# Causal attention with relative bias on the paired helpers, in a two-block fp32 transformer kernel

## The chip, the cores and the metric

The kernel runs on one core of one Trainium2 chip. The metric is device time in microseconds of one execution of the whole program; the figure for a kernel is the median of its runs.

## What is computed

Two transformer blocks of two layers each, over 256 tokens of width 1024 (the first block adds 16 meta tokens), all in fp32. The part that the change touches is the attention of the second block's first layer, named MoBA. With 256 tokens and blocks of 256 its selection of other blocks selects nothing, and what remains is causal attention of 16 heads of width 64 over the own block, with a relative bias:

```python
q, k, v = jnp.split(h @ w_qkv, 3, axis=-1)      # 16 heads of 64
...
l_own = ... jnp.einsum(... qf, k_own) * scale
d_own = t[:, None] - (j_own * BLK + jnp.arange(BLK))[None, :]
b_own = jnp.moveaxis(bias_table[rel_bucket(d_own)].astype(jnp.float32), -1, 0)
l_own = jnp.where((d_own >= 0)[None], l_own + b_own, NEG)
p = jax.nn.softmax(jnp.concatenate([l_sel, l_own], axis=-1), axis=-1)
...
return o @ w_o
```

Around it the layer is `x = x + moba_attention(rms_norm_2(x, g))`, then `x = x + square(relu(rms_norm_2(x, g) @ w_up)) @ w_down`.

## The kernel before

Everything is held transposed: features on the 128 partitions, tokens along the row. A linear layer is cut into output tiles of 128 features. One tile takes its weights as one piece of 128 x 1024, and for each of its eight chunks of 128 input features three matmuls: high part times high part, high times low, low times high (`pe_tile`, lines 304 to 306). `pe_linear` runs the tiles of one layer; the table `LINEARS` is the order of all layers, and each engine runs through it in that order (`ORDER`).

Weights go through a ring of four slots. SyncE loads a piece into `raw`; ACT rounds it to `w_hi` (`act_round`, line 256), which needs the piece four before it to be used up by PE (`piece_used`); DVE computes the remainder `w_lo` (`dve_rest`, line 265); then PE may use it. While tile t is computed, ACT and DVE prepare piece t + 3. Results lie in four PSUM banks in turn (`tile_bank`), and a tile waits until DVE has read the tile that had its bank (`evac_done`).

In a layer that ends in a residual (`RESID`, such as `moba_out`) DVE does, for each tile t: remainder of piece t + 3, add of tile t to `h` (`dve_resid`, line 429), `x_lo` of tile t - 1. ACT does, for each tile: rounding of piece t + 3, then `x_hi` of tile t (`act_resid`, `act_x_hi`, line 378). GpSimd sums squares for the next norm. The next layer's first tile takes its chunks as their `x_lo` arrives.

`moba_in` is the layer of queries, keys and values: 24 tiles, and tiles 3p, 3p + 1, 3p + 2 are the queries, keys and values of heads 2p and 2p + 1, stored by DVE to `qm`. The attention is woven into these tiles by `att_pe`, `att_dve` and `att_act` (class `Attend`), head by head: in step u PE computes the scores of head u (line 1281), one or two projection tiles (`MOBA_SIDES`), the transposes of the probabilities of head u - 2 (line 1241) and the values of head u - 3 (line 1266). Between, DVE adds the bias and takes the maximum (line 1325), ACT computes the exponentials (line 1376), DVE multiplies by the reciprocal sum (lines 1340, 1343), and ACT copies the transposes to `pt_m` (line 1394). Value rows are transposed once a pair (line 1934) into the free half of bank 6 and copied by ACT (line 1913). After every second head ACT writes `y_hi` (line 1407) and DVE `y_lo` (line 1361), the inputs of the output projection `moba_out`. The scores use banks 5 and 7, the transposes bank 4, the values bank 6. When the 24 tiles are used up, scores of heads 14 and 15 and what follows them run with no tile beside them, and `moba_out` begins behind the last values.

The first block's sliding-window attention (`swa_in`, `pe_swa`) uses another set of helpers, class `Pairs`: the two heads of a pair lie on partitions 0 to 63 and 64 to 127, and their scores are issued alternately, into banks 2 and 3 (`pair_scores`, line 1448); so are their values, into the two halves of the partitions of bank 6 (`pair_values`, line 1470). Its projection tiles use two banks, 0 and 1. In the last step it computes the first six chunks of two tiles of its output projection ahead (`SWA_EARLY`).

## Times and profile before

| | us |
|---|---|
| median of 3 runs | 1376.86 (1376.09 to 1377.64) |
| the profiled execution | 1382.77 |
| its span | 1381.0, granted TensorE clock 0.966 |
| PE busy, DVE busy, ACT busy in it | 1305.0, 898.7, 660.9 |

The profile is of one execution. The page gives for each engine how long it was busy, the chain of work that ended last, and the costliest groups of instructions by line. The trace behind it can be asked for the instructions of an engine in order of time, and for the busy time and granted clock of a stretch. PE shows overlapping matmuls: the distance of their starts is what one costs, not their duration. An fp32 matmul stands as two records. The stage of the change runs from 744 us, where `moba_in` starts, to 858 us, where `moba_out` starts, and `moba_out` ends at 885 us.

### The profile page before, as it was taken

How to read it: one execution, taken by the hardware profiler on the slowest of the kernel's cores; microseconds unless marked ns; L12 is line 12 of the kernel's file. 1: busy time of each engine (PE TensorE's matmuls, PEld its weight loads, DVE VectorE, ACT ScalarE, POOL GpSimd, SP SyncE). 2: the span in 40 equal slices, each digit the busy share in tenths (PEclk: the TensorE clock that was granted, in tenths of full speed). 3: DMA queues.
4: the chain of work that ended last, by engine and by line, in shares of the span. 5: the costliest groups of instructions: out<-in, count | busy, mean ns of one | idle time of the engine just before them, and what ended most of it. 6: DMA issues, size and time to landing. Idle time of an engine off the chain costs nothing.

```text
span 1381.0 us, 27358 instructions
## 1 busy us (share of the span) xinstructions
PE 1305.0 (94%) x10217; PEld 1245.8 (90%) x10217; DVE 898.7 (65%) x1681; ACT 660.9 (48%) x1148; POOL 185.2 (13%) x233
## 2 busy tenths in 40 slices
PE   7988989999999989999999998999999878999996
PEld 6968979999999869899999986999999766999996
DVE  6956337887755675888755664777555687776553
ACT  5544224555533554655544443555444266555431
POOL 4112213000012222000011000300011123200011
PEclk9979989999999998999999998999999999999998
DMA  6423804555654312555656432565556521555551
GB/s 232 155 90 67 133 16 137 173 178 169 207 176 136 108 62 92 178 185 183 207 190 199 138 122 74 159 189 187 184 185 195 181 68 33 181 183 184 187 191 64
DMA packets 60354, 206.31 MB, mean 149 GB/s; under 512 B 6000, under 2 KB 14320, under 8 KB 60144
## 3 DMA queue, kind: packets, MB, share of 16 engines
q1 hardware_dynamic: 56000, 200.81, 46.1%
q10 hardware_dynamic: 4272, 4.35, 1.0%
q8 instruction: 58, 0.95, 0.3%
q14 instruction: 24, 0.20, 0.0%
HBM read 200.95 MB, written 4.19 MB: 149 GB/s over the span
## 4 chain that ended last, share of the span: by engine, by line
PE 83%; DVE 10%; ACT 4%; issue 3%; POOL 1%; DMA 0%; DVEq 0%; POOLq 0%; ACTq 0%
PE bank L304 24%; PE bank L306 24%; PE bank L305 24%; DVE w_lo L265 3%; ACT w_hi L256 2%; DVE cb L635 1%; PE bank L1266 1%; PE bank L1078 1%; PE bank L1281 1%; PE bank L1094 1%; PE bank L1032 1%; PE bank L1092 1%; DVE sm_d L1325 1%; PE bank L1241 1%; DVE x_lo L383 1%
## 5 line engine op out<-in xcount | busy, mean ns | idle before, releaser
L265 DVE TENSOR_TENSOR w_lo<-raw,w_hi 128x1024 fp32r<-128x1024 f32 (+1 forms) x358 | 458.8, 1282 | 244.3 <-ACT w_hi L256 244.1
L256 ACT ACTIVATE w_hi<-raw 128x1024 fp32r<-128x1024 f32 (+1 forms) x358 | 388.2, 1085 | 315.7 <-PE bank L306 292.6
L304 PE MATMUL bank<-x_hi,w_hi 128*128 128x256 f32 (+2 forms) x1784 | 519.9, 291 | 18.3 <-DVE x_lo L383 13.9
L306 PE MATMUL bank<-x_hi,w_lo 128*128 128x256 f32 (+2 forms) x1784 | 511.4, 287 | 0.0
L305 PE MATMUL bank<-x_lo,w_hi 128*128 128x256 f32 (+2 forms) x1784 | 511.2, 287 | 0.0
L304 PEld LDWEIGHTS bank<-x_hi,w_hi 128*128 128x128 f32 x1784 | 341.1, 191 | 28.3 <-DVE w_lo L265 11.8
L306 PEld LDWEIGHTS bank<-x_hi,w_lo 128*128 128x128 f32 x1784 | 341.4, 191 | 0.0
L305 PEld LDWEIGHTS bank<-x_lo,w_hi 128*128 128x128 f32 x1784 | 340.7, 191 | 0.3
L304 PE MATMUL bank<-m_hi,w_hi 128*128 128x256 f32 x512 | 143.4, 280 | 0.0
L305 PE MATMUL bank<-m_lo,w_hi 128*128 128x256 f32 x512 | 142.8, 279 | 0.0
L306 PE MATMUL bank<-m_hi,w_lo 128*128 128x256 f32 x512 | 142.8, 279 | 0.0
L304 PE MATMUL bank<-a_hi,w_hi 128*128 128x272 f32 (+1 forms) x352 | 100.1, 284 | 0.0
L305 PE MATMUL bank<-a_lo,w_hi 128*128 128x272 f32 (+1 forms) x352 | 99.9, 284 | 0.0
L306 PE MATMUL bank<-a_hi,w_lo 128*128 128x272 f32 (+1 forms) x352 | 99.8, 284 | 0.0
L304 PE MATMUL bank<-y_hi,w_hi 128*128 128x256 f32 (+2 forms) x312 | 93.3, 299 | 4.9 <-DVE y_lo L2026 1.7
L306 PEld LDWEIGHTS bank<-m_hi,w_lo 128*128 128x128 f32 x512 | 96.3, 188 | 0.0
L304 PEld LDWEIGHTS bank<-m_hi,w_hi 128*128 128x128 f32 x512 | 96.1, 188 | 0.0
L305 PEld LDWEIGHTS bank<-m_lo,w_hi 128*128 128x128 f32 x512 | 95.7, 187 | 0.0
L378 ACT ACTIVATE x_hi<-h,prm 128x272 fp32r<-128x272 f32 x64 | 32.7, 521 | 125.2 <-DVE h L429 125.2
L305 PE MATMUL bank<-y_lo,w_hi 128*128 128x256 f32 (+2 forms) x312 | 91.6, 294 | 0.0
L306 PE MATMUL bank<-y_hi,w_lo 128*128 128x256 f32 (+2 forms) x312 | 91.3, 293 | 0.0
L397 POOL TENSOR_TENSOR acc<-h 128x272 f32<-128x272 f32 x9 | 5.8, 642 | 637.2 <-DVE h L429 631.9
(298 smaller groups left out, 1767.2 us busy)
## 6 DMA issues: line engine op xcount, KB each, us to landing
raw<-w_up SPq DMA_DIRECT2D x88, 512.0 KB, 3.5
raw<-w_mlp_up SPq DMA_DIRECT2D x64, 512.0 KB, 4.3
raw<-w_mlp_down SPq DMA_DIRECT2D x64, 512.0 KB, 4.1
raw<-w_down SPq DMA_DIRECT2D x32, 704.0 KB, 4.0
raw<-w_mix_in SPq DMA_DIRECT2D x29, 512.0 KB, 3.5
raw<-w_moba_in SPq DMA_DIRECT2D x24, 512.0 KB, 3.5
raw<-w_swa_in SPq DMA_DIRECT2D x12, 512.0 KB, 3.5
raw<-w_mix_out SPq DMA_DIRECT2D x8, 512.0 KB, 3.9
```

The source lines that it names most:

```text
L256: nc.scalar.activation(w_hi[:, slot, 0:WIDTHS[g]], raw[:, slot, 0:WIDTHS[g]], ACT.Copy).then_inc(hi_ready, 1)
L265: nc.vector.tensor_tensor(w_lo[:, slot, 0:WIDTHS[g]], raw[:, slot, 0:WIDTHS[g]], w_hi[:, slot, 0:WIDTHS[g]].bitcast(F32), ALU.subtract).th ...
L304: nc.tensor.matmul(out, whi, xh, start=(chunk == 0), stop=False)
L305: nc.tensor.matmul(out, whi, xl, start=False, stop=False)
L306: mm = nc.tensor.matmul(out, wlo, xh, start=False, stop=end)
L378: nc.scalar.activation(x_hi[:, c, :], h[:, c, :], ACT.Copy, scale=norm_w(name, c)).then_inc(x_hi_ready, 1)
L383: nc.vector.scalar_tensor_tensor(out=x_lo[:, c, :], in0=h[:, c, :], scalar=norm_w(name, c), in1=x_hi[:, c, :].bitcast(F32), op0=ALU.mult, ...
L635: nc.vector.scalar_tensor_tensor(out=cb[:, t % 2, :], in0=g[:, tap:tap + T], scalar=dn_w(tap, t + 4 * i), in1=cb[:, t % 2, :], op0=ALU.mul ...
L1032: nc.tensor.matmul(BC[b % 4][:, 0:T], ident[0:rows, col:col + 1].to_broadcast([rows, P]), (ba if b < 8 else l2r)[0:rows, :], start=True, s ...
L1078: mm = nc.tensor.matmul(pbank[0:c, hs], bt[0:c, n, hs], xm_of(n)[0:c, hs], start=True, stop=True)
L1092: nc.tensor.matmul(half(INV_BANKS[n][1][0:c, hs], level, 0), xt_of(n)[0:c, hs], half(p[0:c, hs], level, 0), start=True, stop=True)
L1094: mm = nc.tensor.matmul(half(yt_bank(n)[0:c, hs], level, 1), p[0:c, hs], half(xt_of(n)[0:c, hs], level, 1), start=True, stop=True)
```

## The change

The class of MoBA's attention changes from `Attend` to `Pairs`, and the engines' code for `moba_in` is written out on the paired helpers.

- `tile_bank`: the tiles of `moba_in` use two banks, 0 and 1, in place of four; a tile waits for the read of the tile two before it.
- Eight steps, one a pair. PE: scores of both heads, transposes of the pair's value rows (now in bank 7), two tiles, transposes of both heads' probabilities of the same pair, one tile, values of both heads.
- DVE: bias and maximum of both heads, `y_lo` of the pair before, read of the first tile, normalisation of both heads, then remainders and reads of the other tiles. ACT: `y_hi` of the pair before, value rows, exponentials of both heads, two roundings, two copies of transposes, one rounding.
- The last step has no tiles of `moba_in`. There PE computes seven of eight chunks (`MOBA_EARLY`) of tiles 0, 1 and 2 of `moba_out` between the parts of the attention; `pe_linear` adds the eighth chunk of each, then goes on with tile 3.

```diff
-            if lin is LIN["swa_in"]:
+            if lin in (LIN["swa_in"], LIN["moba_in"]):
                 return bank[(lin.tile0 + t) % 2]
...
-                behind = 2 if lin is LIN["swa_in"] else BANKS
+                behind = 2 if lin in (LIN["swa_in"], LIN["moba_in"]) else BANKS
...
-            begun = 2 if name == "swa_out" else 0
+            begun, chunk = {"swa_out": (2, SWA_EARLY), "moba_out": (3, MOBA_EARLY)}.get(name, (0, 0))
             for t in range(begun):
-                pe_tile(pe, lin, t, ready=ready if t == 0 else None, part=(SWA_EARLY, KD))
+                pe_tile(pe, lin, t, ready=ready if t == 0 else None, part=(chunk, KD))
...
-            att_dve(dve, moba, tile=tile)
+            for p in range(HEADS // 2):
+                t = 3 * p + 3
+                more = t < lin.tiles
+                pair_reduce(dve, moba, p)
+                if p:
+                    pair_low(dve, moba, p - 1)
+                if more:
+                    tile(t)
+                pair_norm(dve, moba, p)
+                if more:
+                    rest(t)
+                    tile(t + 1)
+                    rest(t + 1)
+                    rest(t + 2)
+                    tile(t + 2)
+            pair_low(dve, moba, HEADS // 2 - 1)
...
+            round_(0)
+            act_std(act, name)
+            round_(1)
+            round_(2)
+            for p in range(HEADS // 2):
+                t = 3 * p + 3
+                more = t < lin.tiles
+                if p:
+                    pair_high(act, moba, p - 1)
+                act.wait_ge(S("mv_turned"), p + 1)
+                nc.scalar.activation(vrow_m[:, :, p * P:(p + 1) * P],
+                                     bank[7][:, 0:SEQ].rearrange("p (c k) -> p c k", c=2),
                                      ACT.Copy).then_inc(S("mv_ready"), 1)
...
+                pair_exps(act, moba, p)
+                if more:
+                    round_(t)
+                    round_(t + 1)
+                pair_copies(act, moba, p)
+                if more:
+                    round_(t + 2)
+            pair_high(act, moba, HEADS // 2 - 1)
...
+            def value_turn(p):
+                pe.wait_ge(evac_done, lin.tile0 + 3 * p + 3)
+                if p:
+                    pe.wait_ge(S("mv_ready"), p)
...
-            att_pe(pe, moba, tile=lambda t: pe_tile(pe, lin, t), rows=rows)
+            for p in range(HEADS // 2):
+                t = 3 * p + 3
+                pe.wait_ge(evac_done, lin.tile0 + 3 * p + 2)
+                pair_scores(pe, moba, p)
+                value_turn(p)
+                if t < lin.tiles:
+                    pe_tile(pe, lin, t)
+                    pe_tile(pe, lin, t + 1)
+                    pair_turn(pe, moba, p)
+                    pe_tile(pe, lin, t + 2)
+                    pe.wait_ge(S("mv_ready"), p + 1)
+                    pair_values(pe, moba, p)
+                else:
+                    pe_tile(pe, out, 0, ready=early, part=(0, MOBA_EARLY))
+                    moba.wait(pe, "max", 2 * HEADS)
+                    pe_tile(pe, out, 1, part=(0, MOBA_EARLY))
+                    pair_turn(pe, moba, p)
+                    pe_tile(pe, out, 2, part=(0, 4))
+                    pe.wait_ge(S("mv_ready"), p + 1)
+                    pair_values(pe, moba, p)
+                    pe_tile(pe, out, 2, part=(4, MOBA_EARLY))
```

PE's row at the change of one pair to the next, before (values of head 0, value rows of the second pair, transposes of head 1, scores of head 4, then a tile):

```order
L1266 MATMUL bank<-pt_m,vrow_m 64x256
L1266 MATMUL bank<-pt_m,vrow_m 64x128
L1934 MATMUL bank<-cst,qm 128x128 x2
L1241 MATMUL bank<-cst,sm_m 128x128 x3
L1281 MATMUL bank<-qm 128x256
L1281 MATMUL bank<-qm 128x128
L304 MATMUL bank<-x_hi,w_hi 128x256
```

The same place in the changed kernel:

```order
L1470 MATMUL bank<-pt_m,vrow_m 64x256 x2
L1470 MATMUL bank<-pt_m,vrow_m 64x128 x2
L1448 MATMUL bank<-qm 128x256 x2
L1448 MATMUL bank<-qm 128x128 x2
L1955 MATMUL bank<-cst,qm 128x128 x2
L304 MATMUL bank<-x_hi,w_hi 128x256
```

Values and scores now stand for two heads each, side by side, once in three tiles; the six transposes (line 1460) stand alone between the second and third tile.

DVE's row in one step of the changed kernel, from the second head's scores on (1515 is `y_lo`, 1884 and 1888 read a tile, 265 is a weight remainder):

```order
L1493 TENSOR_SCALAR st_m<-st_m 128x2
L1515 TENSOR_TENSOR y_lo<-bank,y_hi 128x256
L1884 SCALAR_TENSOR_TENSOR qm<-bank,rstd 128x256
L1500 RECIPROCAL st_m<-st_m 128x2
L1509 TENSOR_SCALAR sm_m<-sm_m,st_m 128x256
L1509 TENSOR_SCALAR sm_m<-sm_m,st_m 128x128
...
L265 TENSOR_TENSOR w_lo<-raw,w_hi 128x1024
L1888 TENSOR_TENSOR qm<-bank,rstd 128x256
L265 TENSOR_TENSOR w_lo<-raw,w_hi 128x1024 x2
L1888 TENSOR_TENSOR qm<-bank,rstd 128x256
```

And before, in a step with two tiles:

```order
L1331 TENSOR_SCALAR st_m<-st_m 128x2
L1340 RECIPROCAL st_m<-st_m 128x2
L1343 TENSOR_SCALAR sm_m<-sm_m,st_m 128x256
L1343 TENSOR_SCALAR sm_m<-sm_m,st_m 128x128
L1889 SCALAR_TENSOR_TENSOR qm<-bank,rstd 128x256
L265 TENSOR_TENSOR w_lo<-raw,w_hi 128x1024
L1893 TENSOR_TENSOR qm<-bank,rstd 128x256
L265 TENSOR_TENSOR w_lo<-raw,w_hi 128x1024
```

Before, a remainder followed each read; now the read of the first tile stands ahead of both heads' normalisation, and two remainders stand ahead of the read of the third tile.

PE's row behind the last tile of `moba_in`, before, from the scores of head 15 on:

```order
L1281 MATMUL bank<-qm 128x256
L1281 MATMUL bank<-qm 128x128
L1266 MATMUL bank<-pt_m,vrow_m 64x256
L1266 MATMUL bank<-pt_m,vrow_m 64x128
L1934 MATMUL bank<-cst,qm 128x128 x2
L1241 MATMUL bank<-cst,sm_m 128x128 x6
...
L304 MATMUL bank<-y_hi,w_hi 128x256
L305 MATMUL bank<-y_lo,w_hi 128x256
L306 MATMUL bank<-y_hi,w_lo 128x256
```

And now, from the scores of the last pair on:

```order
L1448 MATMUL bank<-qm 128x256 x2
L1448 MATMUL bank<-qm 128x128 x2
L1955 MATMUL bank<-cst,qm 128x128 x2
L304 MATMUL bank<-y_hi,w_hi 128x256
...
L1460 MATMUL bank<-cst,sm_m 128x128 x6
L304 MATMUL bank<-y_hi,w_hi 128x256
...
L1470 MATMUL bank<-pt_m,vrow_m 64x256 x2
L1470 MATMUL bank<-pt_m,vrow_m 64x128 x2
L304 MATMUL bank<-y_hi,w_hi 128x256
```

Matmuls of the output projection (`y_hi`) moved ahead of the last pair's transposes and values: 14 chunks ahead of the transposes, four between them and the values, three behind.

## Rows read from the trace of the kernel before

**Rows 1.** Windows: stretch, its length, busy PE, PEld, DVE, ACT, POOL, clock, DMA

```profile
750.00:840.00 90.00, 90.00 (x668) 81.46 (x667) 56.63 (x160) 44.75 (x101) 0.00 (x0) 1.00 0.43 142
850.00:860.00 10.00, 8.28 (x28) 5.37 (x29) 1.50 (x3) 2.71 (x6) 0.00 (x0) 0.50 0.00 0
555.00:560.00 5.00, 4.26 (x20) 3.69 (x21) 4.07 (x5) 4.18 (x5) 1.61 (x2) 0.75 0.48 137
```

**Rows 2.** PE timeline, one pair's period: start, us, line, idle before

```profile
774.65 0.86 PE L1266 MATMUL bank<-pt_m,vrow_m 128*64 128x256 f32 x4
775.45 0.44 PE L1934 MATMUL bank<-cst,qm 128*128 128x128 f32 x2
...
776.14 0.92 PE L1281 MATMUL bank<-qm 64*128 64x256 f32 x4
776.99 0.39 PE L304 MATMUL bank<-x_hi,w_hi 128*128 128x256 f32 x1
...
779.94 0.49 PE L1241 MATMUL bank<-cst,sm_m 128*128 128x128 f32 x3
...
789.33 0.92 PE L1281 MATMUL bank<-qm 64*128 64x256 f32 x4
```

**Rows 3.** DVE timeline of the output projection: remainders and residual adds

```profile
859.35 1.23 DVE L265 TENSOR_TENSOR w_lo<-raw,w_hi 128x1024 fp32r<-128x1024 f32 x1 [0.52 <-ACT w_hi L256]
862.54 0.43 DVE L429 TENSOR_TENSOR h<-bank,h 128x256 f32<-128x256 f32 x1 [1.97 <-PE bank L306]
864.51 1.23 DVE L265 TENSOR_TENSOR w_lo<-raw,w_hi 128x1024 fp32r<-128x1024 f32 x1 [1.54 <-ACT w_hi L256]
865.65 0.42 DVE L429 TENSOR_TENSOR h<-bank,h 128x256 f32<-128x256 f32 x1
...
884.72 0.41 DVE L429 TENSOR_TENSOR h<-bank,h 128x256 f32<-128x256 f32 x1
```

**Rows 4.** PE timeline behind both output projections, the sliding-window one first

```profile
555.57 0.39 PE L304 MATMUL bank<-x_hi,w_hi 128*128 128x258 f32 x1 [2.54 <-DVE x_lo L383]
...
558.26 0.41 PE L304 MATMUL bank<-x_hi,w_hi 128*128 128x256 f32 x1
558.90 0.41 PE L304 MATMUL bank<-x_hi,w_hi 128*128 128x256 f32 x1
...
885.60 0.39 PE L304 MATMUL bank<-x_hi,w_hi 128*128 128x256 f32 x1 [1.12 <-DVE x_lo L383]
```

**Rows 5.** PE timeline in the sliding-window stage: paired values, scores, transposes

```profile
476.46 0.87 PE L1470 MATMUL bank<-pt_s,vrow 128*64 128x256 f32 x8
477.26 0.70 PE L1767 MATMUL bank<-ptx,vmbd 128*128 128x256 f32 x2
477.89 0.97 PE L1448 MATMUL bank<-qs 64*128 64x272 f32 x8
478.79 0.88 PE L1460 MATMUL bank<-cst,sm_s 128*128 128x128 f32 x6
479.51 0.38 PE L1762 MATMUL bank<-cst,smx 128*128 128x128 f32 x2
...
505.30 0.97 PE L1448 MATMUL bank<-qs 64*128 64x272 f32 x8
```

**Rows 6.** PE timeline: start of projection tile 2, last chunk of tile 23

```profile
750.00 0.28 PE L304 MATMUL bank<-x_hi,w_hi 128*128 128x256 f32 x1
...
840.11 0.28 PE L304 MATMUL bank<-x_hi,w_hi 128*128 128x256 f32 x1
```

**Rows 7.** DVE timeline: a sliding-window pair's last normalisation, read of tile 0

```profile
510.07 0.54 DVE L1509 TENSOR_SCALAR sm_s<-sm_s,st_s 128x256 f32<-128x256 f32 x2
...
749.77 0.42 DVE L1889 SCALAR_TENSOR_TENSOR qm<-bank,rstd 128x256 f32<-128x256 f32 x1
```

**Rows 8.** ACT timeline: the last y_hi and the rounding behind it

```profile
857.99 0.38 ACT L1407 ACTIVATE y_hi<-bank 128x256 fp32r<-128x256 f32 x1 [1.63 <-PE bank L1266]
858.27 1.05 ACT L256 ACTIVATE w_hi<-raw 128x1024 fp32r<-128x1024 f32 x1
```

More of the change, by code:

```diff
@@ L1844, in build @@
             ("qm", [P, 24, SEQ]), ("vrow_m", [P, 2, D]), ("bias_m", [P, HEADS, 2 * P]),
-            ("sm_m", [P, 3, 3 * P]), ("pt_m", [P, 2, 3 * P]), ("st_m", [P, HEADS, 10])], u_at)
+            ("sm_m", [P, 4, 3 * P]), ("pt_m", [P, 2, 2, 3 * P]), ("st_m", [P, HEADS, 8])], u_at)
         CAUSAL_TURNS = ((4, 0, P, 2 * P), (4, P, P, 0), (4, 2 * P, P, P))
-        MOBA_SIDES = {}
-        for pair in range(1, HEADS // 2):
-            MOBA_SIDES[2 * pair - 2] = (3 * pair, 3 * pair + 1)
-            MOBA_SIDES[2 * pair - 1] = (3 * pair + 2,)
-        moba = Attend(
-            "moba", "moba_out", 2 * P, P,
-            lambda u, r, g: qm[r, u // 2, P * g:P * (g + 1)],
-            lambda u, r, g: qm[r, 8 + u // 2, 0:P * (g + 1)],
-            lambda u, chunk, c: vrow_m[:, chunk, u * HD:(u + 1) * HD],
-            lambda u: bias_m[:, u, :], lambda u: bias_m[:, u, P:2 * P], CAUSAL_TURNS,
-            (sm_m, pt_m, st_m), MOBA_SIDES)
+        MOBA_EARLY = 7
+        moba = Pairs(
+            "moba", "moba_out", 2 * P, P, 0, 0,
+            lambda p, r, g: qm[r, p, P * g:P * (g + 1)],
+            lambda p, r, g: qm[r, 8 + p, 0:P * (g + 1)],
+            lambda p, j, chunk: vrow_m[:, chunk, (2 * p + j) * HD:(2 * p + j + 1) * HD],
+            lambda u: bias_m[:, u, :], lambda u: bias_m[:, u, P:2 * P], lambda u, x: 1.0,
+            (sm_m, pt_m, st_m))
         def load_bias(act, dst):
@@ L1894, in tile, with rest @@
                                             ALU.mult).then_inc(evac_done, 1)
+            def rest(t):
                 dve_rest(dve, lin.piece0 + t + AHEAD)
@@ L1906, in act_moba, with round_ @@
             lin = LIN[name]
-            def tile(t):
+            def round_(t):
                 act_round(act, lin.piece0 + t + AHEAD)
-            def rows(pair):
-                act.wait_ge(S("mv_turned"), pair + 1)
-                nc.scalar.activation(vrow_m[:, :, pair * P:(pair + 1) * P],
-                                     bank[6][:, SEQ:2 * SEQ].rearrange("p (c k) -> p c k", c=2),
-                                     ACT.Copy).then_inc(S("mv_ready"), 1)
-            tile(0)
-            act_std(act, name)
@@ L1919, in act_moba @@
-            tile(1)
-            tile(2)
-            att_act(act, moba, tile, rows)
+            round_(0)
[10 more added lines that the diff above has]
+                                     bank[7][:, 0:SEQ].rearrange("p (c k) -> p c k", c=2),
+                                     ACT.Copy).then_inc(S("mv_ready"), 1)
+                pair_exps(act, moba, p)
[5 more added lines that the diff above has]
+                    round_(t + 2)
@@ L1923, in pe_moba @@
+            pair_high(act, moba, HEADS // 2 - 1)
         def pe_moba(pe, name):
             lin = LIN[name]
-            def rows(pair):
-                pe.wait_ge(evac_done, lin.tile0 + 3 * pair + 3)
-                if pair >= 1:
-                    pe.wait_ge(S("mv_ready"), pair)
-                if pair >= 2:
-                    pe.wait_ge(y_lo_ready, Y0["moba_out"] + pair - 1)
+            out = LIN["moba_out"]
+            def value_turn(p):
+                pe.wait_ge(evac_done, lin.tile0 + 3 * p + 3)
+                if p:
+                    pe.wait_ge(S("mv_ready"), p)
@@ L1933, in rows, with early @@
                 for c in range(2):
-                    tr = nc.tensor.transpose(bank[6][:, SEQ + c * P:SEQ + (c + 1) * P],
-                                             qm[:, 16 + pair, c * P:(c + 1) * P], ident)
+                    tr = nc.tensor.transpose(bank[7][:, c * P:(c + 1) * P],
+                                             qm[:, 16 + p, c * P:(c + 1) * P], ident)
                 tr.then_inc(S("mv_turned"), 1)
+            def early(c):
+                pe.wait_ge(y_lo_ready, Y0["moba_out"] + c + 1)
```

1 line of the change is left out of this document (added).

## The prediction

> **What bounds the kernel now.** Read the stretches of the windows view first. While the MoBA input projection and its attention run together, the other engines have room and PE is never idle: between 750 and 840 us it is busy 90.00 of 90.00 us [rows 1]. So in that stretch each matmul taken off PE is time taken off the kernel. Then the 24 projection tiles are used up, and what is left of the attention is a chain with nothing beside it: from 850 to 860 us PE is busy 8.28 of 10 us, at a granted clock of 0.50, which is its 1.2 GHz level [rows 1].
>
> Read next the PE timeline of one pair of heads [rows 2]. A projection tile is 24 matmuls and takes 2.95 us when it follows attention work (776.99 to 779.94), some 0.1 of that for the change of kind; 2.84 is the tile. The scores of one head take 0.85 (776.14 to 776.99), its values 0.80 (774.65 to 775.45). A pair repeats every 13.19 us (776.14 to 789.33).
>
> Last read DVE in the output projection [rows 3]. From the first residual add at 862.54 to the last at 884.72 are 22.18 us for seven steps, 3.17 each, while a PE tile takes 2.84. The loop goes residual add, x_hi and weight rounding on ACT, weight remainder on DVE, next residual add; PE is only its guest, and at 885.60 it waited 1.12 us for x_lo [rows 4]. So behind the attention it is not PE's work that counts, but **when this loop starts**.
>
> **Stage one, the pairs.** Sliding-window attention in this kernel already runs the paired helpers. There the scores of two heads take 0.90 us with 272+144 columns (477.89 to 478.79), and the values of two heads take 0.80, as much as one head's here [rows 5]. Scaled by columns, the paired scores with 256+128 take 0.84; 0.90 is the other end. From the end of projection tile 2 (752.85) to the end of tile 23 (the last chunk starts at 840.11 [rows 6], plus 0.36, so 840.47) PE has 87.62 us. What changes of it, counted from the code's steps:
> - scores: 14 single heads at 0.85 become 7 pairs at 0.84: 11.90 - 5.88 = 6.0 less.
> - values: 10 single heads at 0.80 become 6 pairs at 0.80: 3.2 less.
> - transposes of the probabilities: 33 become 42, at about 0.12 each (six take 0.7 in the paired stage): 1.1 more. One more pair of value-row transposes (0.28): 0.3 more.
> - changes between projection and attention: 20 runs of tiles become 14, each change costs about 0.19 (0.1 in, as above, and 0.1 out): 1.1 less.
> - **two banks instead of four**: tile 2 must now wait until DVE has read tile 0. DVE does that from 749.77 for 0.42, and PE started tile 2 at 750.00 [rows 6, 7]; 0.3 more, once. Later tiles find their bank read: tiles t and t+2 lie 5.7 us apart.
>
> Sum: 6.0 + 3.2 - 1.1 - 0.3 + 1.1 - 0.3 = 8.6, so tile 23 ends at about 831.8. The pair's period should fall from 13.19 to 11.3.
>
> What could take this back is the order on DVE and ACT, which now serve a pair in one go. Count from the start of a pair's scores. In the paired stage, probabilities of both heads are ready 5.3 us after it (505.30 to 510.07, plus 0.54) [rows 5, 7]. Here DVE must first read tile t, which PE ends at 4.1, then normalises two heads (1.4): ready at about 6.0, and PE comes to the transposes at 6.95. Slack 0.9. The value-row transposes of the next pair wait for the third tile, which DVE reads after two remainders; that is about 11.1, and PE asks at 12.2. Slack 1.1. I cost both at nothing; past that slack each microsecond is paid seven times.
>
> Here the Trainium skill speaks against the change: "TensorEngine Tiling (Array Packing)", section "PSUM Bottleneck", says that packing speeds up TensorE but not the reading of PSUM, which may become the limit. By that rule the step would be paced by DVE. A DVE step here is 7.9 us of work, from the durations above, in an 11.3 us period, so I give the rule only the chance of the stall rival below.
>
> **Stage two, the tail.** Before, tile 23 ends at 840.47 and the first residual add starts at 862.54 [rows 3]: 22.07 us, with single heads in turn and much of it at the lower clock [rows 1]. After, count from the end of tile 23: values of pair 6 until 0.9, scores of pair 7 until 1.7, value rows until 2.1, seven of eight chunks of output tile 0 (7 x 0.355) until 4.7, of output tile 1 until 7.2, transposes until 7.9, four chunks of tile 2 until 9.4, values until 10.3. The probabilities of pair 7 are due 0.9 + 5.3 = 6.2 and hide behind output tile 1; y_lo of pair 6 is due about 3.8 and is wanted at 4.3. ACT then writes y_hi (10.5) and rounds weight piece 3 (10.8), as it does 0.28 us apart before [rows 8]; DVE starts its remainder 1.08 after the rounding (858.27 to 859.35 [rows 3, 8]), 11.9, and from one remainder to the next start are 1.14 (864.51 to 865.65 [rows 3]): **first residual add at 13.0**. Output tile 0 itself is done at 11.6, so the loop waits for the remainder, no longer for PE. That is 22.07 - 13.0 = 9.1 less.
>
> From there all runs at 3.17 a step as before, because the loop is DVE's and ACT's: PE ends output tile 7 at 28.6 and the last add falls at 35.2. The early chunks of the output projection therefore bring only that PE is out of the way; they do not shorten the loop.
>
> **What it gives back.** PE is ahead of the loop by more than before. It will wait about 2.4 us for x_lo of chunk 5 and 2.8 for chunk 6 of the next projection, where it waited 1.12. After sliding-window attention, where the same loop left a gap of 2.54 us, chunks came 0.64 apart (558.26 to 558.90) instead of 0.355 (2.84 over 8), at the 1.2 GHz level; the granted clock of 555 to 560 us was 0.75 [rows 1, 4]. Some six chunks at that pitch cost 1.8 us, and they are lost, since PE bounds the MLP that follows. I take 1.8; ends 0 and 2.4.
>
> **Sum.** 8.6 + 9.1 - 1.8 = 15.9 less. Against the profiled execution, 1382.77 us (its span 1381.0 and 1.77 around it), that is 1366.9. It lies 5.9 above the median of the runs, 1376.86, and I take the offset to stay: 1376.86 - 15.9 = **1361.0 us**.
>
> **Rivals.**
> - **No loss of clock** behind the output projection: for it, a gap of 1.12 before cost nothing; against it, the 2.54 gap of the sister stage did. 17.7 less: 1359.2.
> - **Steps stall.** DVE's order (read tile t, normalise, remainder, read, two remainders, read) is in-order, and slacks of 0.9 and 1.1 are small beside three or four semaphore hops and an exp that starts late. If each of the seven steps loses 1 us, 8.9 less: 1368.0. For it: the row order of DVE; against it: DVE and ACT have some 3 and 5 us free in each step.
> - **The two halves don't overlap here.** Then scores keep 0.85 a head and values 0.80: 14 x 0.85 + 12 x 0.80 against 5.88 + 4.8 takes back 10.8 until tile 23; another 2.5 come in the tail (0.8, 0.9 and 0.8), and 1361.0 becomes 1374.3. Against it: the same lines and banks do overlap in the paired stage [rows 5].
> - **Slower.** One mechanism: the value-row transposes and the second tile after them wait for DVE to read tile 3p+5, behind two weight remainders that wait for ACT's roundings, and those for the copies of the transposes. To be slower by over 0.2% it must eat 15.9 + 2.8 = 18.7 us, 2.7 in each of seven steps on top of the slack of 1.1: the read must come 3.8 us after its place. Time from there on 1379.6. Nothing in the loads of DVE and ACT asks for this.
>
> **Chances.** Forecast (within 2 us) 0.66; no loss of clock 0.13; stalls 0.13; no overlap 0.04; slower 0.02; the rest, 0.02, no difference. The forecast's own spread comes from paired scores between 0.84 and 0.90 (0.4 us), clock 0 to 2.4, and a few tenths for each change of kind. The range from 1357.5 to 1367.5 holds the first two cases and the milder stalls. A measurement of this kernel tells about 0.2% (2.8 us) from no change; faster 0.96, same 0.02, slower 0.02.
>
> **What would show it.** The pair's period on PE 11.3 us, no PE idle time between 750 and 832; paired scores 0.84 for eight records; tile 2 starting at 750.3; the first residual add 13.0 us after tile 23, with weight remainder and not PE as what it waited for; adds 3.17 apart; two PE waits for x_lo over 2 us each, then 0.64 between chunks. The forecast is wrong if PE waits inside the steps for DVE's reads or for normalised probabilities, or if the granted clock falls before the tail.

## The result, and the profile after

| | before | after |
|---|---|---|
| median, us | 1377.25 (1376.09 to 1380.92, 4 runs) | 1360.5 (1358.24 to 1364.26, 4 runs) |
| profiled execution, its span | 1382.77, 1381.0 | 1364.26, 1362.4 |
| granted TensorE clock | 0.966 | 0.967 |

Ratio 0.9864, 95% interval 0.9834 to 0.9893: 1.4% faster. Forecast was 1361.0.

Windows of after, columns as in [rows 1]; the first stretch is the eight steps, the others the output projection:

```profile
750.00:832.00 82.00, 82.00 (x707) 77.43 (x706) 58.55 (x170) 46.31 (x108) 0.00 (x0) 1.00 0.50 156
842.00:862.00 20.00, 17.60 (x137) 16.56 (x138) 12.43 (x19) 9.58 (x14) 8.96 (x12) 1.00 0.52 160
862.00:870.00 8.00, 5.46 (x24) 4.99 (x23) 5.95 (x7) 4.90 (x6) 2.50 (x4) 0.60 0.56 183
```

PE has no idle time in the steps. DVE is busy 58.55 of 82 us, ACT 46.31. Before, the stretch from 850 to 860 us ran at a clock of 0.50 with nothing beside the attention [rows 1]; that stretch is gone, and a new one at 0.60 stands behind the output projection.

The PE timeline of one pair, against [rows 2]:

```profile
773.62 0.87 PE L1470 MATMUL bank<-pt_m,vrow_m 128*64 128x256 f32 x8
774.42 0.92 PE L1448 MATMUL bank<-qm 64*128 64x256 f32 x8
775.27 0.44 PE L1955 MATMUL bank<-cst,qm 128*128 128x128 f32 x2
...
781.22 0.82 PE L1460 MATMUL bank<-cst,sm_m 128*128 128x128 f32 x6
...
784.77 0.87 PE L1470 MATMUL bank<-pt_m,vrow_m 128*64 128x256 f32 x8
```

Eight records of values take 0.80 (773.62 to 774.42) and eight of scores 0.85 (to 775.27): as much as four did before. The values of the next pair start 11.15 us later (784.77); the period was 13.19.

The DVE timeline around the first residual adds, against [rows 3], and the PE timeline where the next layer waits, against [rows 4]:

```profile
839.74 0.42 DVE L1515 TENSOR_TENSOR y_lo<-bank,y_hi 128x256 fp32r<-128x256 f32 x1 [4.96 <-ACT y_hi L1535]
840.69 1.22 DVE L265 TENSOR_TENSOR w_lo<-raw,w_hi 128x1024 fp32r<-128x1024 f32 x1 [0.52 <-ACT w_hi L256]
841.83 0.42 DVE L429 TENSOR_TENSOR h<-bank,h 128x256 f32<-128x256 f32 x1
843.78 1.23 DVE L265 TENSOR_TENSOR w_lo<-raw,w_hi 128x1024 fp32r<-128x1024 f32 x1 [1.54 <-ACT w_hi L256]
844.93 0.42 DVE L429 TENSOR_TENSOR h<-bank,h 128x256 f32<-128x256 f32 x1
845.26 0.49 DVE L383 SCALAR_TENSOR_TENSOR x_lo<-h,prm,x_hi 128x272 fp32r<-128x272 f32 x1
846.89 1.30 DVE L265 TENSOR_TENSOR w_lo<-raw,w_hi 128x1024 fp32r<-128x1024 f32 x1 [1.13 <-ACT w_hi L256]
848.11 0.41 DVE L429 TENSOR_TENSOR h<-bank,h 128x256 f32<-128x256 f32 x1
```

```profile
861.69 0.38 PE L304 MATMUL bank<-x_hi,w_hi 128*128 128x256 f32 x1 [1.90 <-DVE x_lo L383]
864.85 0.58 PE L304 MATMUL bank<-x_hi,w_hi 128*128 128x256 f32 x1 [2.54 <-DVE x_lo L383]
...
867.95 0.41 PE L304 MATMUL bank<-x_hi,w_hi 128*128 128x256 f32 x1
868.59 0.41 PE L304 MATMUL bank<-x_hi,w_hi 128*128 128x256 f32 x1
```

The first add (841.83) follows a weight remainder and waits for nothing else. The adds are 3.18 apart (844.93, 848.11). PE waits 1.90 and 2.54 us for `x_lo`, and then takes a chunk every 0.64 us instead of every 0.355.

**How traces are compared from here on.** The same instructions ahead of the stage bring its first matmul at times between 736.97 and 745.35 us in the executions shown below, so two spans can differ by 8 us without any edit. I therefore count from the stage's first matmul (s), from the end of tile 23 (E), and from the start of the norm's matmul behind the output projection (N). These differences repeat to about 0.1 us in the steps. "After" is the changed kernel; a remainder is a weight remainder of DVE (line 265).

| | E - s | first add - E | N - s | end - N | end - s |
|---|---|---|---|---|---|
| before | 96.53 | 22.07 | 143.08 | 493.98 | 637.06 |
| after | 86.52 | 12.52 | 123.66 | 495.95 | 619.61 |

The end is the span, which stands to 0.1 us, so the last two columns are good to 0.05.

So 10.0 us come from the steps, 9.55 from the stretch between tile 23 and the first add, 0.1 is lost until N, and 2.0 are given back behind N. That is 17.45. The span's other 1.15 lie ahead of the stage and are not the change's.

### The profile page after: what moved, and what is told of

Its sections match the earlier page's. It is cut to its first block, busy times and chain, and to the rows that moved or that the text cites. A ratio compares the mean times of both kernels' runs of the same rounds, so it can differ in the third digit from the quotient of the medians.

```text
span 1362.4 us, 27349 instructions
## 1 busy us (share of the span) xinstructions
PE 1289.1 (95%) x10217; PEld 1236.5 (91%) x10217; DVE 898.2 (66%) x1681; ACT 660.0 (48%) x1148; POOL 185.0 (14%) x233
## 4 chain that ended last, share of the span: by engine, by line
PE 82%; DVE 10%; ACT 4%; issue 2%; POOL 0%; DMA 0%; DVEq 0%; POOLq 0%; ACTq 0%
PE bank L304 24%; PE bank L306 24%; PE bank L305 24%; DVE w_lo L265 3%; ACT w_hi L256 2%; DVE cb L635 1%; PE bank L1078 1%; PE bank L1448 1%; PE bank L1470 1%; PE bank L1032 1%; PE bank L1094 1%; PE bank L1460 1%; DVE h L429 1%; PE bank L1092 1%; DVE sm_d L1325 1%
```

## The experiments

"Before" was measured again beside each group of runs; its median was 1380.07, 1379.02 and 1380.43 us in the three groups. Three kernels were executed once each: they are read by their traces, not by their time. The recorded expectations call the runs by number: the second is the one without the early projection, the fourth the one that rounds ahead, the seventh the loop with the add first.

### The changed kernel again

> The changed kernel once more, as the measure for the three beside it. Seconds of the stage as in its first trace: attention steps 11.15 us apart, tile 23 of moba_in 86.5 us after the start of tile 0, first residual add of moba_out 12.5 us after that, next add 3.17 apart, resumption of PE at the next projection at half clock. Median 1358 to 1363.

Measured: 1364.33 us (1358.9 to 1367.28, 6 runs), ratio 0.9882 (0.9856 to 0.9907). E - s is 86.52, the first add 12.52 behind E, N - s 123.66, end - N 496.11: the first trace repeated in every part.

### Without the early output projection

```diff
-            begun, chunk = {"swa_out": (2, SWA_EARLY), "moba_out": (3, MOBA_EARLY)}.get(name, (0, 0))
+            begun, chunk = {"swa_out": (2, SWA_EARLY)}.get(name, (0, 0))
...
-                    pe_tile(pe, out, 0, ready=early, part=(0, MOBA_EARLY))
                     moba.wait(pe, "max", 2 * HEADS)
-                    pe_tile(pe, out, 1, part=(0, MOBA_EARLY))
                     pair_turn(pe, moba, p)
-                    pe_tile(pe, out, 2, part=(0, 4))
...
-                    pe_tile(pe, out, 2, part=(4, MOBA_EARLY))
```

> The changed kernel without the output projection begun early: in the last step only transposes and values, then moba_out from tile 0. Theory (the tail is worth what it does to the start of the residual loop): values of the last pair come 1.6 us sooner, y_hi at 8.4 instead of 10.0 after tile 23, but tile 0 must then be computed whole and, if the clock falls in the idle stretch as it did in the kernel before, ends at about 13.5; first add at 11.2 (clock holds) or 13.5 (it falls) instead of 12.5. PE is then less ahead of the loop, so the waits for x_lo and the half clock behind them shrink: 1 to 2 us back. Total between 2 us faster and 1 us slower than the changed kernel. Rival (early chunks are worth their PE time, 21 chunks of 0.355): 7.4 us slower.

Measured: 1360.93 us (1359.12 to 1362.8, 5 runs), ratio 0.986 (0.9836 to 0.9885), no slower than with the early chunks. N - s is 123.20, end - N 493.93, end - s 617.13. The DVE timeline shows what the first add now waits for:

```profile
837.98 1.23 DVE L265 TENSOR_TENSOR w_lo<-raw,w_hi 128x1024 fp32r<-128x1024 f32 x1 [0.52 <-ACT w_hi L256]
840.70 0.42 DVE L429 TENSOR_TENSOR h<-bank,h 128x256 f32<-128x256 f32 x1 [1.49 <-PE bank L306]
```

The last `y_hi` comes 8.11 behind E instead of 10.01, since PE has nothing to put between. PE's first output tile is then computed whole, and much of it at half clock: with PE idle for part of the tail, the granted clock falls to 0.50.

```profile
835.50:838.80 3.30, 3.30 (x18) 2.84 (x15) 1.24 (x2) 1.33 (x2) 0.00 (x0) 0.50 0.00 0
```

The add falls 12.19 behind E against 12.52. PE's waits for `x_lo` are 1.08 and 0.19, as in the kernel before (1.12 and 0.18), and behind the output projection the clock holds. So the early chunks, the part of the change that reads like its reward, cost 2.5 us in these traces (0.46 until N, 2.0 behind it). Nor are the 9.55 us of the tail theirs: without them PE starts the output projection 8.0 behind E (836.51), where before it started 17.4 behind (857.88). It is the last step in pairs that shortened the tail.

### Filler matmuls in the two gaps

```diff
                 if name in NORMS:
+                    if name == "mlp_up0" and c in (5, 6):
+                        for _ in range(4 if c == 5 else 5):
+                            nc.tensor.matmul(bank[7][:, 0:256], C("ones"), ..., start=True, stop=True)
                     pe.wait_ge(x_lo_ready, 8 * NORMS[name] + c + 1)
```

> The changed kernel with nine matmuls of constants into an unused bank while PE would wait for x_lo of chunks 5 and 6 of mlp_up0 (four, then five, 0.45 us each, in gaps of 1.9 and 2.5 us); they compute nothing that is used. Theory (the gaps let the clock fall, and that costs 1.8 us): chunks behind the gap 0.355 apart instead of 0.64, from the resumption to the end 495.5 us instead of 497.5, total 1.8 us less. Rival (slow chunks come from something else, such as the norm's matmul or DMA): 0.64 stays, no change or 0.3 us more.

Measured: 1361.83 us (1357.6 to 1366.39, 6 runs), ratio 0.9875 (0.985 to 0.9899). PE timeline and windows:

```profile
853.86 1.89 PE L327 MATMUL bank<-cst 128*128 128x256 f32 x8
855.86 0.39 PE L304 MATMUL bank<-x_hi,w_hi 128*128 128x256 f32 x1
856.33 2.32 PE L327 MATMUL bank<-cst 128*128 128x256 f32 x10
...
861.34 0.28 PE L304 MATMUL bank<-x_hi,w_hi 128*128 128x256 f32 x1
861.69 0.28 PE L304 MATMUL bank<-x_hi,w_hi 128*128 128x256 f32 x1
```

```profile
855.00:860.00 5.00, 4.31 (x21) 3.08 (x20) 3.47 (x7) 2.87 (x4) 2.74 (x4) 1.00 0.48 137
860.00:865.00 5.00, 5.00 (x39) 4.74 (x40) 4.45 (x4) 3.64 (x7) 0.40 (x1) 1.00 0.57 188
```

With PE at work in the gaps the granted clock stays at 1.00 (2.4 GHz) and the chunks are 0.35 apart again. What that is worth is read at the weight remainders of DVE behind N, counted from N:

| remainder behind N | before | no early chunks | after | filler |
|---|---|---|---|---|
| the 67th | 189.29 | 189.28 | 191.01 | 189.28 |
| the 76th | 235.74 | 235.70 | 236.58 | 235.50 |
| the 77th | 277.41 | 277.38 | 279.40 | 278.78 |
| end | 493.98 | 493.93 | 495.95 | 495.35 |

At the 67th, at the end of the MLP, the filler has taken back 1.73 us and stands where before stands. **Behind N the clock loss costs 1.73 us.** It costs another 0.18 ahead of N, which falls 2.48 behind the last residual add in after and 2.30 with the filler or before. Yet at the end only 0.6 of it is left. The rest goes in the DSA stage, where the clock falls in every one of these kernels, but not at the same places nor for as long. Between the 67th and the 76th after is 0.9 us quicker than before (45.57 against 46.45), at a granted clock of 0.86 in the 12 us from N + 200 where before had 0.72. Between the 76th and the 77th it is slower. That place in windows, from N + 246, of before, after, the filler kernel and the one without early chunks:

```profile
1133.02:1139.02 6.00, 4.57 (x31) 3.01 (x29) 5.79 (x26) 4.65 (x19) 3.86 (x7) 1.00 0.01 3
```

```profile
1112.45:1118.45 6.00, 5.33 (x22) 3.05 (x20) 5.75 (x27) 4.12 (x15) 3.85 (x7) 0.53 0.01 3
```

```profile
1106.45:1112.45 6.00, 5.34 (x18) 3.18 (x20) 5.76 (x25) 3.94 (x15) 3.75 (x7) 0.51 0.02 5
```

```profile
1111.17:1117.17 6.00, 5.42 (x26) 3.29 (x26) 5.69 (x25) 4.41 (x17) 3.67 (x7) 0.72 0.01 3
```

Before keeps 1.00 there; after and the filler kernel fall to 0.53 and 0.51, and lose 1.2 and 1.6 us; without early chunks the mean is 0.72 and nothing is lost (41.68 against 41.67). The code there is the same in all four, and PE's busy time in the 6 us just ahead does not tell them apart: 2.93 us before, 2.64 in after, 2.98 in the other two. What tips it stays open.

### Rounding ahead, values first

Weight piece 3 is rounded and its remainder taken ahead of the last `y_hi` and `y_lo`; only two output tiles are begun early, with 7 + 3 chunks ahead of the values.

```diff
-            begun, chunk = {"swa_out": (2, SWA_EARLY), "moba_out": (3, MOBA_EARLY)}.get(name, (0, 0))
+            begun, chunk = {"swa_out": (2, SWA_EARLY), "moba_out": (2, MOBA_EARLY)}.get(name, (0, 0))
...
+                if not more:
+                    act_round(act, LIN["moba_out"].piece0 + AHEAD)
                 pair_copies(act, moba, p)
...
+            dve_rest(dve, LIN["moba_out"].piece0 + AHEAD)
             pair_low(dve, moba, HEADS // 2 - 1)
...
-                    pe_tile(pe, out, 1, part=(0, MOBA_EARLY))
                     pair_turn(pe, moba, p)
-                    pe_tile(pe, out, 2, part=(0, 4))
+                    pe_tile(pe, out, 1, part=(0, 3))
...
-                    pe_tile(pe, out, 2, part=(4, MOBA_EARLY))
+                    pe_tile(pe, out, 1, part=(3, MOBA_EARLY))
```

The output projection's own loop leaves piece 3 out of its first round.

> The changed kernel with the last step in another order: weight piece 3 of moba_out is rounded and its remainder taken before the last y_hi and y_lo, and PE does seven chunks of output tile 0, transposes, three chunks of tile 1, values, four chunks of tile 1; tile 2 isn't begun. Theory (the start of the residual loop counts): values end at 8.3 instead of 9.9 after tile 23, the loop waits for output tile 0 alone, first add at 10.4 instead of 12.5, total 2.1 us less. Rival (PE's own work bounds the output projection): seven chunks more of PE work left behind the values, no gain or up to 2.5 us slower.

Measured: 1357.47 us (1355.2 to 1363.3, 6 runs), ratio 0.9846 (0.9821 to 0.9872). The first add falls 9.96 behind E instead of 12.52, N - s is 121.09 (2.57 less), end - s 616.63 (3.0 less). When the loop starts is what counts, as the prediction said, and nearly all of it arrives at N.

### Heads one after the other

```diff
-            for g, c0, w in ((1, 0, at.wa), (0, at.wa, at.wb)):
-                for j in range(2):
+            steps = [(g, c0, w, j) for g, c0, w in ((1, 0, at.wa), (0, at.wa, at.wb)) for j in range(2)]
+            if at.name == "moba":
+                steps.sort(key=lambda x: x[3])
```

and the same in `pair_values`.

> The MoBA pair's scores and values are issued head after head instead of alternately; numbers of matmuls, banks, waits and everything else are those of after. Theory (the paired form pays because neighbouring matmuls of two heads sit in different halves of the array and run side by side): only the junction between the heads can still overlap (128 of 384 columns). Scores of a pair rise from 0.85 to about 1.4 us (two single heads at 0.85 are 1.70, less one matmul's overlap), values from 0.80 to about 1.35; a pair's period rises from 11.15 to about 12.25; tile 23 ends 8 x 0.55 + 7 x 0.55 = 8 us later, about 95 us after the stage's start instead of 86.5; the tail has one values and no scores more: +1; time of after plus 8 to 10, about 1369 to 1371. Rival (the pair is cheap because fewer waits and changes of kind lie between its matmuls, not because the heads run side by side): the scores stay at 0.85 and the time is that of after. Second rival: with the shorter projection runs beside DVE and ACT, the longer pair is hidden: cannot be while PE is busy 82.00 of 82 us.

Measured: 1360.25 us (1359.14 to 1363.16, 4 runs), ratio 0.9862 (0.983 to 0.9893): no slower. The expectation of +8 to 10 us was wrong. The PE timeline of a step, then two windows of one group of scores:

```profile
783.03 0.88 PE L1476 MATMUL bank<-pt_m,vrow_m 128*64 128x256 f32 x8
783.84 0.93 PE L1451 MATMUL bank<-qm 64*128 64x256 f32 x8
784.70 0.44 PE L1961 MATMUL bank<-cst,qm 128*128 128x128 f32 x2
```

```profile
772.67 0.49 PE L1451 MATMUL bank<-qm 64*128 64x256 f32 x2
...
773.21 0.40 PE L1451 MATMUL bank<-qm 64*128 64x128 f32 x4
```

The scores still take 0.86. Two records of 256 columns start at 772.67, where a single head of the kernel before shows one:

```profile
776.14 0.48 PE L1281 MATMUL bank<-qm 64*128 64x256 f32 x1
```

The records of 128 columns, four of them, follow from 773.21 on for both heads together. In the program the first head's 128-column matmul stands ahead of the second head's 256-column one. So by these starts the second head does not wait for its turn in the program; it runs as soon as its half of the array is free. Either the pair is cheap for that reason, or for one that has nothing to do with halves. The next two runs tell these apart.

The Trainium skill, "TensorE: Matmul & The Clock Gate", section "The mechanism", says that matmuls start and end strictly in program order, and only weight loads are pulled ahead. These starts differ from that, and the unchanged period (11.17 against 11.15 us) speaks with them.

### Both heads in the same half, and whole-array work between the heads

```diff
-                    r = slice(HD * j, HD * j + HD)
+                    r = slice(HD * j, HD * j + HD) if at.name != "moba" else slice(0, HD)
```

> After, but the scores of both heads of a MoBA pair read the lower 64 rows of q and k (so the second head computes the first one's scores; same number, shape, banks and order of matmuls). Theory (heads run side by side because they sit in different halves of the array's rows, and the array lets a matmul of a free half start although it was issued behind the other half's, as the run with the heads apart made likely): now there is one half and the two heads go one after the other: scores of a pair 1.70 us instead of 0.85, period 12.0 instead of 11.15, tile 23 ends 8 x 0.85 = 6.8 us later, 93.3 after the stage's start instead of 86.52; the tail (pair 7's own scores are in the 8) unchanged. Rival (eight records of small matmuls take 0.85 for a reason that has nothing to do with the rows, for instance because a group of four only pays a fixed cost): period stays 11.15.

```diff
+                    if between and (g, j) == (1, 1):
+                        between(p)
...
-                pair_scores(pe, moba, p)
-                value_turn(p)
+                pair_scores(pe, moba, p, between=value_turn)
```

> After, but in each MoBA pair the two transposes of the value rows, which use the whole array, stand between the scores of head one and of head two (before: head, head, transposes). Theory A (a matmul passes earlier ones only while these leave its half free; a matmul of all rows closes the door in both directions): scores can't overlap: 0.85 + 0.20 + 0.85, period 12.0, tile 23 at 93.3 from the stage's start. Theory B (the overlap is no matter of what stands between): period 11.15 and 86.5.

PE timelines, of the same-half kernel first:

```profile
795.80 1.57 PE L1448 MATMUL bank<-qm 64*128 64x256 f32 x8
797.30 0.44 PE L1955 MATMUL bank<-cst,qm 128*128 128x128 f32 x2
...
806.82 0.87 PE L1470 MATMUL bank<-pt_m,vrow_m 128*64 128x256 f32 x8
```

```profile
790.35 0.87 PE L1475 MATMUL bank<-pt_m,vrow_m 128*64 128x256 f32 x8
791.15 0.92 PE L1453 MATMUL bank<-qm 64*128 64x256 f32 x4
792.00 0.44 PE L1960 MATMUL bank<-cst,qm 128*128 128x128 f32 x2
792.36 0.92 PE L1453 MATMUL bank<-qm 64*128 64x256 f32 x4
...
802.52 0.87 PE L1475 MATMUL bank<-pt_m,vrow_m 128*64 128x256 f32 x8
```

In one half the scores of a pair take 1.50 us, not 0.85; a period is 11.82, and E - s is 91.16 (4.64 more, 6.8 expected). One execution: 1364.83 us, in an execution whose stage starts at 739.22, 3.6 earlier than in after. This kernel leaves out the second head's scores: it computes the first head's twice. With the two transposes between, each head takes 0.85 again and the transposes 0.36 instead of 0.20; a period is 12.17, and E - s is 93.61 (7.1 more, 6.8 expected). One execution: 1374.12 us, of which 1.4 are a later start of the stage than in the profiled run of before.

Both together settle it for the scores. Heads in different halves run side by side, in any order among themselves, and work on the whole array between them ends that. They also divide the 0.85 us of a single head: 1.50 for two in one half and 0.85 for one make 0.65 for the head and 0.20 for the change of kind in front of it. So of what pairing saves on a pair of scores, 0.65 is the overlap and 0.20 one change of kind less. For the values, whose halves are columns (128*64 in the rows), the runs show only that two heads take the 0.80 of one, in either order; no run put both in one half.

The Trainium skill, "TensorEngine Tiling (Array Packing)", section "Key Properties", says just this: tiles of the array run independently, and a change of tiling mode drains the engine. The traces agree, with 0.65 and 0.20 us beside it.

### Two banks in the kernel before

```diff
-            if lin is LIN["swa_in"]:
+            if lin in (LIN["swa_in"], LIN["moba_in"]):
                 return bank[(lin.tile0 + t) % 2]
...
-                behind = 2 if lin is LIN["swa_in"] else BANKS
+                behind = 2 if lin in (LIN["swa_in"], LIN["moba_in"]) else BANKS
```

> Before, with nothing changed but that the tiles of the MoBA input projection go round two banks instead of four (so tile 2 waits for the read of tile 0, and so on). Theory: only tile 2 waits. Its start, and the first pair's scores with it, come 0.3 us later (scores 9.30 us after the stage's first matmul instead of 8.99), and the end of tile 23 comes 0.3 later, at 96.8 instead of 96.53 from the stage's start; everything else as before, time +0.3. Rival: in the single-head form the side tiles stand closer to DVE's reads, so tiles inside the steps wait too: PE idle between 750 and 840 us, and tile 23 more than 1 us later.

Measured, one execution: 1381.4 us. The first scores come 9.32 behind s instead of 8.99, E - s is 96.83 instead of 96.53, N - s 143.34 instead of 143.08. PE has no idle time inside the steps:

```profile
750.00:839.00 89.00, 89.00 (x659) 80.46 (x658) 55.20 (x158) 43.72 (x100) 0.00 (x0) 1.00 0.45 139
```

Two banks cost 0.3 us, once, as predicted.

### The loop with the add first

The loop of 3.18 us can be read off after's DVE rows and the ACT timeline beside them: add (844.93), `x_hi` 0.45 later, rounding 0.43 after that, remainder 1.08 after that (846.89), next add 1.22 later (848.11). That is a ring, and it closes because DVE takes the remainder ahead of the add.

```diff
             for t in range(lin.tiles):
-                for q in range(lin.per_tile):
-                    dve_rest(dve, lin.piece0 + t * lin.per_tile + q + AHEAD)
+                if not late:
+                    rests(t)
                 wait_tile(dve, lin, t)
                 nc.vector.tensor_tensor(h[:, t, a:a + n], tile_bank(lin, t)[:, 0:n], ...)
                 if t and nxt != "final":
                     dve_x_lo(dve, nxt, t - 1)
+                if late and t < lin.tiles - 1:
+                    rests(t)
...
+            if late:
+                rests(lin.tiles - 1)
```

`late` is true for `moba_out` alone, and `rests(t)` is the loop that was taken out.

> After, with one change: in the MoBA output projection DVE does the residual add and x_lo of a tile first and the weight remainder behind them (before and after do the remainder first). Theory (the loop of 3.18 us is a ring of ACT and DVE: add 0.45 until x_hi starts, x_hi 0.43 until the rounding, rounding 1.08 until the remainder, remainder 1.22 until the next add, sum 3.18): without the remainder ahead of the add the ring is cut, and PE's 2.85 us a tile set the pace. The first add no longer waits for the remainder either but for PE's tile 0 (about 1.3 earlier in both). Adds 2.85 apart, seven steps 2.3 less; norm matmul 2.3 to 3.5 us earlier from the stage's start, about 120.5 instead of 123.66. PE's waits for x_lo: both shorter, sum about 2 instead of 4.4; if so the clock holds and another 1.7 is won from the norm matmul to the MLP; if the clock falls all the same, not. Time: after less 2.3 to 5. Rival: PE is not fast enough at the remainders (the later remainder delays tile t+3 of PE) or ACT's rounding sets 3.18 on its own: adds stay 3.18 apart, time of after.

Measured: 1355.48 us (1350.84 to 1358.98, 6 runs), ratio 0.9821 (0.9794 to 0.9848). DVE timeline and, below, a window of the loop:

```profile
845.13 0.41 DVE L437 TENSOR_TENSOR h<-bank,h 128x256 f32<-128x256 f32 x1
845.47 0.67 DVE L383 SCALAR_TENSOR_TENSOR x_lo<-h,prm,x_hi 128x272 fp32r<-128x272 f32 x1
846.07 1.66 DVE L265 TENSOR_TENSOR w_lo<-raw,w_hi 128x1024 fp32r<-128x1024 f32 x1
847.65 0.41 DVE L437 TENSOR_TENSOR h<-bank,h 128x256 f32<-128x256 f32 x1
```

```profile
843.10:858.10 15.00, 15.00 (x128) 15.00 (x129) 15.00 (x20) 8.94 (x13) 14.06 (x13) 1.00 0.63 198
```

The ring is cut, and the adds are 2.5 apart (845.13, 847.65), closer than PE's 2.84: the early tiles lie ready, and DVE itself, busy 15.00 of 15.00, sets the pace to the end of the loop. N - s is 117.08 (6.58 less than after), no wait for `x_lo` is left, the clock holds, and end - N is 493.72 (2.2 less). The expectation was 2.3 to 3.5 less until N; more came because it had PE's 2.84 as the pace, and the next run shows what the early chunks have to do with that.

> The kernel of the seventh run (MoBA output projection: residual add first, remainder behind) without the early chunks of the output projection, so with the second run it completes a square of two edits. With the old loop the early chunks brought nothing (-2.5 us from the stage's start to the end without them). Theory (early chunks shorten PE's work behind the attention, which counts only where the loop does not set the pace): now PE does: its first output tile can start about 8.1 after tile 23 and 8 tiles of 2.84 follow, 22.7, so the last add falls at about 86.5 + 31.2 = 117.7 from the stage's start and the norm matmul at 120.2, 3.1 later than with early chunks (117.08). POOL and DVE then have gaps and the remainder takes less than 1.66. The clock holds in both. Time: the seventh run's plus 3 (1358.5). Rival (the early chunks are worthless in any loop): norm matmul at 117 and the seventh run's time.

This is the edit of the second run and that of the seventh together. Measured: 1359.85 us (1354.49 to 1366.88, 6 runs), ratio 0.9871 (0.9849 to 0.9894). In its DVE timeline every add waits for PE, 2.84 apart:

```profile
841.28 0.42 DVE L437 TENSOR_TENSOR h<-bank,h 128x256 f32<-128x256 f32 x1 [0.43 <-PE bank L306]
...
844.12 0.42 DVE L437 TENSOR_TENSOR h<-bank,h 128x256 f32<-128x256 f32 x1 [0.43 <-PE bank L306]
```

N - s, as a square of two edits:

| | old loop | add first |
|---|---|---|
| with early chunks | 123.66 | 117.08 |
| without | 123.20 | 121.05 |

Early chunks bring nothing while the ring of DVE and ACT paces the loop (+0.46), and 3.97 us once it is cut. Against the lower left, early chunks alone lose 0.46, the add first alone gains 2.15, and both gain 6.12. The expectation was 3.1 for the right column, with the clock held. It did not hold: from 830.0 to 833.3, while PE waits for the last pair and begins its first output tile, the granted clock is 0.50, as in the second run. So part of what early chunks bring is that they keep PE at work there.

### All of it, in all four loops

The fourth run's order, and the add first in the output projections of mixer, sliding-window attention, MoBA and DSA.

> The version of the fourth run (weight piece 3 rounded and its remainder taken ahead of the last y_hi and y_lo; output tiles 0 and 1 begun early, values ahead of the rest), and in all four loops with one projection tile per residual add (mixer, sliding-window, MoBA and DSA output projections, each now at 3.18 a step) DVE adds first and takes the weight remainder behind. Theory of the ring: each loop runs at PE's 2.85: 4 x 7 x 0.33 = 9.2 less than the fourth run's, which lay about 3 below after: after less 12, about 1349. Where a loop then ends with PE waiting less for x_lo, a clock loss behind it may go as well (up to 1.7 at two places): down to 1346. Rival: ACT's or PE's order paces the loops: they stay at 3.18 and the time is that of the fourth run.

Measured: 1346.46 us (1344.78 to 1352.0, 6 runs), ratio 0.9771 (0.9744 to 0.9798): faster than before and after. From first to last add the mixer's loop takes 21.36 us instead of 22.48, the sliding-window one 17.91 instead of 22.17, DSA's 19.88 instead of 22.17; N - s is 116.51. No wait of PE for `x_lo` is left behind any of them. A window of MoBA's loop:

```profile
831.00:852.00 21.00, 21.00 (x180) 21.00 (x179) 16.98 (x24) 12.04 (x17) 16.72 (x15) 1.00 0.54 168
```

PE is busy 21.00 of 21.00: here it is PE's work that counts again.

## Why the prediction was right, point by point

- **Steps**: 8.6 predicted, 10.0 measured. Scores 0.85 (0.84), values 0.80 (0.80) and the period 11.15 (11.3) are as worked out. Between the end of tile 2 and E, by PE's starts, scores give 5.8 (6.0 predicted) and values 3.2 (3.2). The 42 transposes of the probabilities take 4.0 where 33 took 3.6: 0.4 more, not 1.1, since six take 0.57 (770.07 to 770.64 in after) where I took 0.12 each. The value rows, seven times 0.20 against six times 0.28, give 0.3 back where I added 0.3. Projection tiles with the changes around them, the bank wait aside, give 1.4 (1.1). That is the missing 1.4: 0.7 of transposes, 0.6 of value rows and 0.3 of changes, less 0.2 of scores. The mis-sized terms are the small ones.
- **Two banks**: 0.3 predicted, 0.3 in after and 0.3 alone.
- **Slacks on DVE and ACT**: held. In the seventh step DVE ends the normalisation 0.9 before PE comes to the transposes, and the third tile is read 1.1 before the value rows: the 0.9 and 1.1 of the prediction. No PE idle time in 82 us, so the rival of stalling steps did not come. Nor did DVE pace the step, as it would by the rule that the prediction takes from the Trainium skill, "TensorEngine Tiling (Array Packing)", section "PSUM Bottleneck": it was busy 58.55 of 82 us.
- **First residual add**: 13.0 behind E predicted, 12.52 measured, with the remainder and not PE in front of it. Tail -9.1 predicted, -9.55 measured. The list was 0.5 too long by the last `y_hi` (10.01 behind E, not 10.5), through value rows, transposes and changes of kind as above; from there to the add it holds to 0.01.
- **Early chunks do not shorten the loop**: right, and sharper than said: without them the kernel is not slower. The square shows that this rests on the ring.
- **Clock**: waits of 2.4 and 2.8 predicted, 1.90 and 2.54 measured; 1.8 us predicted, 1.73 measured where the filler isolates it. With the 0.18 ahead of N the filler prices the loss at 1.9. The 2.0 at the end of the trace are the 1.73 and 0.3 of the DSA stage, where after gains 0.9 and loses 1.2; nothing of that was in the prediction. The rival without a loss of clock is refuted for this kernel by 0.64 us a chunk.
- **No overlap**: refuted by the pair's 0.85, and with its reason by the same-half run. The size I gave that rival (0.85 a head, 10.8 until E) would have been too high by the 0.20 of each change of kind: 1.50 a pair, not 1.70.
- **Slower**, by the third tile's read: its slack of 1.1 was untouched.
- **Sum**: 15.9 predicted, 17.45 found in the traces; the medians differ by 16.75, and by 15.74 in the next group (1380.07 and 1364.33). That the median of after fell within 0.5 us of the forecast is in part luck: 1.1 us of upstream drift and the runs' spread (6 us in four runs) are as large as the terms I discuss. The terms are better tested by the traces than by the median.

What stays open: what decides for how long the clock falls at the two places of the DSA stage, worth 0 to 1.6 us between the 76th and the 77th remainder in these traces.

## What to carry to other kernels

In these traces two heads' matmuls, each on half of the array, cost what one head's cost if they lie in different halves and nothing that uses the whole array stands between; how the heads are interleaved among themselves did not matter. Before giving an engine a head start, look for the ring that paces the next loop: here early output tiles were worth -0.5 us behind a ring of DVE and ACT and 4.0 once one line was moved to cut it. An engine that gets ahead of a loop can also lose: PE's longer waits cost it the clock, 1.9 us here.

## What the runs showed of the hardware

With the heads issued one after the other, the second head's 256-column matmul started ahead of the first head's 128-column one, against program order: at 772.67 and 773.21.

DVE and GpSimd slow each other where they overlap. In after's steps, with GpSimd idle, a remainder takes 1.22 us. In the seventh run's loop, with GpSimd busy 14.06 of 15 us, it takes 1.66; GpSimd's own accumulation grows in the same place:

```profile
844.21 1.63 POOL L400 TENSOR_TENSOR acc<-acc,sq 128x272 f32<-128x272 f32 x1
```

```profile
846.33 0.77 POOL L400 TENSOR_TENSOR acc<-acc,sq 128x272 f32<-128x272 f32 x1
```

The first row is of the seventh run, the second of after. The overlap alone is not enough: over the trace of after the 260 remainders of 128x1024 with no GpSimd instruction beside them take 1.20 to 1.23, the 66 with one take 1.20 to 1.82. In the seventh run it sets the 2.5 us of the loop; with 1.22 a step would have been about 2.0, an estimate from the rows of after. The Trainium skill, "GPSIMD Engine Reference", section "1. Specifications", says that GpSimd's SBUF interfaces are shared with VectorE, with contention for DVE instructions with two SBUF inputs; the remainder is one, and both durations agree with that.
